# Another order of places for the first expert-row gathers, and what is moved for it

## The reference, cut to what matters

```
mod = silu(c) @ w_ada + b_ada                      # 6 vectors of 1024: ..., gate2 is the last
h2  = rms_norm(x, norm2_w) * (1 + scale2) + shift2
per token and head (8 heads): q = h2 @ peer_wq     # 2 halves of 128
  s = scores of each half against 128 keys; top 16 of each half
  combo = top16_a + top16_b (16 x 16); top 16 of it -> 16 expert numbers, g = softmax
  u_sel, v_sel = peer_u[expert], peer_v[expert]    # rows of 1024 each
  a = gelu(u_sel . h2);  y += sum_k (g * a)_k v_sel_k
x = x + gate2 * y
```

## Time and profile before

| | |
|---|---|
| median of 3 runs | 1178.29 us (1177.71 to 1179.69) |
| the profiled execution | 1180.36 us, its span 1178.4 us |
| TensorE, VectorE, ScalarE, POOL busy | 89%, 71%, 37%, 23% of the span |
| gathers (queue q0) | 36864 packets, 268.45 MB, 55.0% of the 16 engines' span |
| mean granted TensorE clock | 0.972 |

### The profile page before, as it was taken

One profiled execution on the slowest core, in us unless ns is written; L12 is line 12 of the kernel. 1 busy time (PEld: TensorE's weight loads), 2 busy tenths in 40 slices (PEclk: granted clock), 3 DMA queues, 4 the chain that ended last, 5 costly groups with the idle time before them and its releaser, 6 DMA issues.

```text
span 1178.4 us, 18884 instructions
## 1 busy us (share of the span) xinstructions
PE 1051.1 (89%) x7587; PEld 980.2 (83%) x7587; DVE 837.5 (71%) x1801; ACT 433.0 (37%) x913; POOL 268.8 (23%) x289
## 2 busy tenths in 40 slices
PE   8999987999999987777877778878999999999997
PEld 6999986998899877777877777778899888898886
DVE  7978889667667667666776766655756868765776
ACT  3635832123212221222122122211557654476452
POOL 1000005343334333333333333434000000300000
PEclk9999999999999999998999999989999999999999
DMA  9965988999999999999999999999854655455540
GB/s 371 406 244 180 348 313 307 420 421 420 421 420 420 421 420 421 420 421 420 420 420 421 420 421 422 420 422 420 325 208 161 237 205 184 147 211 179 186 171 36
DMA packets 59480, 390.35 MB, mean 331 GB/s; under 512 B 6785, under 2 KB 7809, under 8 KB 15618
## 3 DMA queue, kind: packets, MB, share of 16 engines
q0 software_dynamic: 36864, 268.45, 55.0%
q1 hardware_dynamic: 21056, 120.10, 27.8%
q10 hardware_dynamic: 1474, 0.60, 0.2%
HBM read 388.08 MB, written 1.05 MB: 330 GB/s over the span
## 4 chain that ended last, share of the span: by engine, by line
PE 63%; DMA 24%; DVE 6%; ACT 4%; issue 1%; SPq 0%; another core or an unknown queue 0%; DVEq 0%; ACTq 0%
DMA rows<-in_peer_uv,work 23%; PE aux L1566 23%; PE pj L1609 6%; PE pj L1611 5%; PE pj L1610 5%; PE aux L1545 5%; PE pj L1286 5%; PE pj L1287 4%; PE pj L1288 4%; DVE rows L2061 2%; DMA rows<-in_w_ada 1%; PE aux L1360 1%; ACT work L1142 1%; ACT rows L1010 1%; PE aux L1425 1%
## 5 line engine op out<-in xcount | busy, mean ns | idle before, releaser
L1566 PE MATMUL aux<-work,rows 128*128 128x128 f32 x2080 | 263.4, 291 | 73.8 <-ACT work L1142 73.8
L1566 PEld LDWEIGHTS aux<-work,rows 128*128 128x128 f32 x2080 | 256.2, 206 | 81.6 <-ACT work L1142 81.4
L1566 PE MATMUL aux<-work,low_pairs 128*128 128x128 f32 x2016 | 238.2, 279 | 30.2 <-ACT work L1142 30.1
L1566 PEld LDWEIGHTS aux<-work,low_pairs 128*128 128x128 f32 x2016 | 233.0, 195 | 34.0 <-ACT work L1142 34.0
L898 POOL DMA_INDIRECT rows<-in_peer_uv,work x130 | 125.5, 965 | 301.2 <-PE aux L1566 232.1
L707 DVE TENSOR_TENSOR wlo<-wring,whi 128x1024 fp32r<-128x1024 f32 x100 | 121.0, 1235 | 77.6 <-ACT whi L701 77.1
L898 POOL DMA_INDIRECT low_pairs<-in_peer_uv,work x126 | 118.3, 939 | 158.5 <-PE aux L1566 153.4
L1286 PE MATMUL pj<-xh,whi 128*128 128x256 f32 x512 | 146.3, 286 | 0.4
L1137 ACT ACTIVATE work<-work 128x4 f32<-128x4 f32 (+2 forms) x71 | 14.7, 207 | 358.3 <-DVE work L2061 358.3
L1287 PE MATMUL pj<-xl,whi 128*128 128x256 f32 x512 | 144.8, 283 | 0.0
L1288 PE MATMUL pj<-xh,wlo 128*128 128x256 f32 x512 | 144.8, 283 | 0.0
(11 more groups left out here) (288 smaller groups left out, 1461.5 us busy)
## 6 DMA issues: line engine op xcount, KB each, us to landing
wring<-in_w SPq DMA_DIRECT2D x76, 1024.0 KB, 4.8
rows<-in_w_ada SPq DMA_DIRECT2D x40, 512.0 KB, 10.1
low_pairs<-in_w_ada SPq DMA_DIRECT2D x1, 4096.0 KB, 13.4
rows<-in_w SPq DMA_DIRECT2D x3, 1024.0 KB, 10.4
rows<-in_peer_uv,work POOLq DMA_INDIRECT x130
work<-in_late_rows SPq DMA_DIRECT2D x2, 1024.0 KB, 7.5
xT<-in_gate_rows SPq DMA_DIRECT2D x2, 1024.0 KB, 7.2
rows<-in_norm_rows SPq DMA_DIRECT2D x2, 1024.0 KB, 7.3
```

The source lines that it names most:

```text
L1566: ins = mm(peer_sum[t][:, c * P:(c + 1) * P], pair(n)[:, D + c * P:D + (c + 1) * P], diag[:, n % PICKS, :], start=(n % (EXPERT_HEADS * PIC ...
```

## The change

Every pick gets its place from `slot(n)`. For picks before 240 it is the table FIRST_ORDER, the same permutation in each round of 12: picks 0 to 11 lie in places 0, 1, 6, 7, 2, 3, 4, 8, 9, 10, 11, 5. From pick 240 (`LAST_ROUND`) on it is n % 12 as before. POOL waits, before a pick from 12 on, for the latest earlier pick in the same place (`pick_ahead_in_slot`), and before the first twelve for what their place held: pick 4 for head 0's query, 5 for head 1's, 6 for the key scores of head 1, 7 to 10 for two, four, six and eight of the gate2 tiles, 11 for all of them.

`EARLY_HEADS = 2`: head 1's first tile is computed like head 0's, directly behind it and behind the transposes of h2 (`early_scores_of(1)`); `score_query` and `score_keys` of heads 0 and 1 then compute the second tile alone. VectorE's order becomes route(0), route(1), two gate2 tiles, and then in group 0: after each of the first four dot products one tile, after `weigh` the last two tiles, after the second `weigh` the bias. ScalarE's exponential of group 0 moves from behind head 1's scores to between the query and the scores of head 0's second tile, that of group 1 before the query of head 2.

```diff
--- before.py
+++ after.py
@@ -46,7 +46,7 @@
 LOW_PLACES = 8
 SLOTS, LOW_SLOTS = 12, 6
 PAIRS = SLOTS - LOW_SLOTS
-AHEAD = 2
+AHEAD, EARLY_HEADS = 2, 2
 EXPERTS = 4
 
 
@@ -265,6 +265,21 @@
 LOW_PICKS = LAST_PICK // SLOTS * SLOTS
 WHI_PICKS, WLO_PICKS, XH_PICKS, XL_PICKS = [LOW_PICKS - LOW_SLOTS + n for n in (2, 4, 5, 6)]
 LAST_GROUP = NT * EXPERT_HEADS - 1
+
+FIRST_ORDER = (0, 1, 6, 7, 2, 3, 4, 8, 9, 10, 11, 5)
+LAST_ROUND = LAST_PICK // SLOTS * SLOTS - SLOTS
+
+
+def slot(n):
+
+    return n % SLOTS if n >= LAST_ROUND else FIRST_ORDER[n % SLOTS]
+
+
+def pick_ahead_in_slot(n):
+
+    return max(m for m in range(n - 2 * SLOTS, n) if m >= 0 and slot(m) == slot(n))
+
+
 assert LAST_PICK % SLOTS < PAIRS
 GROUPS_BEFORE = [0]
 for g in range(NT * EXPERT_HEADS):
@@ -433,11 +448,11 @@
         own_place = {OWN_UNIT: own_unit, HELD_QUERY: low_pairs[:, 7, :]} | {n: low_pairs[:, 6, 512 * i:512 * i + 512] for i, n in enumerate(SUB_UNITS)} | \
             {n: flat[:, FIRST_HEADS_AT + 2 * D * i:FIRST_HEADS_AT + 2 * D * i + AT_1[n + 1] - AT_1[n]] for i, n in enumerate(FIRST_HEADS)}
         LAST_ADA = 5 * KC
-        LAST_ADA_SLOT = PAIRS - 1
+        FIRST_QUERY_SLOTS, KEYS_SLOT, CONDITION_SLOT, LAST_ADA_SLOTS = (2, 3), 4, 5, tuple(PAIRS + n for n in range(2, 6))
 
         def pair(n):
 
-            k = n % SLOTS
+            k = slot(n)
             return rows[:, k, :] if k < PAIRS else low_pairs[:, k - PAIRS, :]
 
 
@@ -811,10 +826,10 @@
                 for n in range(N2):
                     unit = N1 + l * N2 + n
                     if l == 0 and n == 1:
-                        sp.wait_ge(pair_loaded[(LAST_PICK - 2) % SLOTS], 16 * ((LAST_PICK - 2) // SLOTS + 1))
+                        sp.wait_ge(pair_loaded[slot(LAST_PICK - 2)], 16 * ((LAST_PICK - 2) // SLOTS + 1))
                     if l == 0 and n == 2:
                         load_rows(vg_rows.rearrange("p l f -> p (l f)"), "vg_rows", 0, vg_rows_loaded)
-                        sp.wait_ge(pair_loaded[LAST_PICK % SLOTS], 16 * (LAST_PICK // SLOTS + 1))
+                        sp.wait_ge(pair_loaded[slot(LAST_PICK)], 16 * (LAST_PICK // SLOTS + 1))
                     if l == 0 and n == 4:
                         sp.wait_ge(routed, NT * EXPERT_HEADS)
                         sp.wait_ge(gate_exp, NT * EXPERT_HEADS)
@@ -887,18 +902,21 @@
                 pool.wait_ge(routed, g + 1)
                 for j in range(PICKS):
                     n = g * PICKS + j
-                    if n in (2, 3):
-                        pool.wait_ge(queries, 2 * n - 2)
-                    if n == 4:
+                    k = slot(n)
+                    if n >= SLOTS:
+                        pool.wait_ge(pair_used, pick_ahead_in_slot(n) + 1)
+                    elif k in FIRST_QUERY_SLOTS:
+                        pool.wait_ge(queries, 2 * FIRST_QUERY_SLOTS.index(k) + 2)
+                    elif k == KEYS_SLOT:
                         pool.wait_ge(expert_scores, 2)
-                    if n == LAST_ADA_SLOT:
+                    elif k == CONDITION_SLOT:
                         pool.wait_ge(last_ada_used, KC)
-                    if n >= SLOTS:
-                        pool.wait_ge(pair_used, n - SLOTS + 1)
+                    elif k in LAST_ADA_SLOTS:
+                        pool.wait_ge(last_ada_used, 2 * LAST_ADA_SLOTS.index(k) + 2)
                     pool.indirect_dma_start(
                         out=pair(n), out_offset=None, in_=a["peer_uv"],
                         in_offset=bass.IndirectOffsetOnAxis(ap=expert[g % EXPERTS][:, j:j + 1], axis=0)) \
-                        .then_inc(pair_loaded[n % SLOTS], 16)
+                        .then_inc(pair_loaded[k], 16)
 
             pool.iota(distance, pattern=[[-1, T]], base=P, channel_multiplier=1).then_inc(bias_iota, 1)
             pool.wait_ge(bias_lin, HEADS)
@@ -1092,7 +1110,7 @@
 
             def score_query(h):
 
-                ts = slice(P if h == 0 else 0, T)
+                ts = slice(P if h < EARLY_HEADS else 0, T)
                 for s in range(2):
                     act.wait_ge(queries, 2 * h + s + 1)
                     if h >= 2:
@@ -1102,28 +1120,36 @@
             def score_out(h):
 
                 act.wait_ge(expert_scores, h + 1)
-                first = 1 if h == 0 else 0
+                first = 1 if h < EARLY_HEADS else 0
                 nc.scalar.copy(s_all[:, h + first * EXPERT_HEADS::EXPERT_HEADS, :],
                                aux[:, h % 2, first * 2 * KEYS:].rearrange("p (n k) -> p n k", k=2 * KEYS)).then_inc(scores_out, 1)
 
+            def early_head(h):
+
+                for s in range(2):
+                    act.wait_ge(early_query, 2 * h + s + 1)
+                    nc.scalar.copy(pq[:, h, s, 0:P], aux[:, 4 + s, 0:P]).then_inc(early_query_out, 1)
+                act.wait_ge(early_scores, h + 1)
+                nc.scalar.copy(s_all[:, h, :], aux[:, h, 0:2 * KEYS]).then_inc(early_scores_out, 1)
+
             shift(0)
-            for s in range(2):
-                act.wait_ge(early_query, s + 1)
-                nc.scalar.copy(pq[:, 0, s, 0:P], aux[:, 4 + s, 0:P]).then_inc(early_query_out, 1)
-            act.wait_ge(early_scores, 1)
-            nc.scalar.copy(s_all[:, 0, :], aux[:, 0, 0:2 * KEYS]).then_inc(early_scores_out, 1)
+            early_head(0)
             shift(1)
+            early_head(1)
 
             def gate_exps(g):
 
                 act.wait_ge(routed, g + 1)
                 nc.scalar.activation(gate[g % EXPERTS], top, ACT.Exp, bias=negtop, accum_out=gate_sum[g % EXPERTS]).then_inc(gate_exp, 1)
 
-            for h in range(AHEAD + 1):
-                score_query(h)
-                score_out(h)
-                if h:
-                    gate_exps(h - 1)
+            score_query(0)
+            gate_exps(0)
+            score_out(0)
+            score_query(1)
+            score_out(1)
+            gate_exps(1)
+            score_query(2)
+            score_out(2)
             def x0_hi(t):
 
                 for c in range(2):
@@ -1553,7 +1579,9 @@
                 pe.wait_ge(queries_out, 2 * h + 2)
                 if h >= 2:
                     pe.wait_ge(scores_out, h - 1)
-                for t in range(1 if h == 0 else 0, NT):
+                if h < EARLY_HEADS:
+                    pe.wait_ge(early_scores_out, h + 1)
+                for t in range(1 if h < EARLY_HEADS else 0, NT):
                     for s in range(2):
                         ins = mm(aux[:, h % 2, (2 * t + s) * KEYS:(2 * t + s + 1) * KEYS], pq[:, h % 2, s, t * P:(t + 1) * P],
                                  w[:, 0, (2 * (h % 2) + s) * KEYS:(2 * (h % 2) + s + 1) * KEYS], start=True, stop=True)
@@ -1567,21 +1595,22 @@
                              start=(n % (EXPERT_HEADS * PICKS) == 0 and c % 4 == 0), stop=False, skip_group_check=True)
                 ins.then_inc(pair_used, 1)
 
-            def early_scores_of_head_0():
-
-                w_wait(pe, UNITS_1.index(queries_of(0)))
-                w = w_slot(UNITS_1.index(queries_of(0)))
+            def early_scores_of(h):
+
+                w_wait(pe, UNITS_1.index(queries_of(h)))
+                w = w_slot(UNITS_1.index(queries_of(h)))
                 for s in range(2):
                     for k in range(KC):
-                        if s == 0:
+                        if h == 0 and s == 0:
                             pe.wait_ge(h_ready, KC + k + 1)
                         ins = mm(aux[:, 4 + s, 0:P], w[:, k, s * P:(s + 1) * P], hT[:, k, 0:P], start=(k == 0), stop=(k == KC - 1))
                     ins.then_inc(early_query, 1)
                 n = UNITS_1.index(keys_of(0))
                 w_wait(pe, n)
                 for s in range(2):
-                    pe.wait_ge(early_query_out, s + 1)
-                    ins = mm(aux[:, 0, s * KEYS:(s + 1) * KEYS], pq[:, 0, s, 0:P], w_slot(n)[:, 0, s * KEYS:(s + 1) * KEYS], start=True, stop=True)
+                    pe.wait_ge(early_query_out, 2 * h + s + 1)
+                    ins = mm(aux[:, h, s * KEYS:(s + 1) * KEYS], pq[:, h, s, 0:P], w_slot(n)[:, 0, (2 * h + s) * KEYS:(2 * h + s + 1) * KEYS],
+                             start=True, stop=True)
                 ins.then_inc(early_scores, 1)
 
             def x_tile(l, t):
@@ -1612,12 +1641,12 @@
                     ins.then_inc(steps, 1)
 
             keep_busy(4, 1)
-            early_scores_of_head_0()
+            early_scores_of(0)
             pe.wait_ge(taken_dve, KC)
             turn_h2(0)
+            early_scores_of(1)
             pe.wait_ge(h_ready, 3 * KC)
             score_query(0)
-            pe.wait_ge(early_scores_out, 1)
             score_keys(0)
             for h in range(1, AHEAD + 1):
                 score_query(h)
@@ -1761,12 +1790,14 @@
                 dve.wait_ge(ada_used, hi)
                 chain.link(v.tensor_tensor(mod[:, lo:hi], mod[:, lo:hi], cols[:, B_ADA + lo:B_ADA + hi], ALU.add))
 
-            def last_ada_tiles():
+            def last_ada_tiles(lo, hi):
```

(21 more changed lines are left out.)

## The result

The changed kernel has a median of 1181.65 us (1179.68 to 1185.29) beside 1179.05 us (1177.56 to 1182.07) for the kernel before on the same chip. The ratio is 1.0022 with a 95% interval of 1.0016 to 1.0029: slower by 2.6 us (1.9 to 3.4) where 2.7 us less was forecast, and above the upper end of the range, 1180.0. Its profiled execution lasted 1180.01 us with a span of 1178.1 us; the one of before had 1180.36 and 1178.4. These two are single executions. They agree within 0.4 us though the medians are 2.6 apart, so the traces show where time went, and the medians how much.

A forecast was written before the change was run, and what follows sets the result against it. The gathers' DMA queue, at a 421 GB/s plateau, was taken to bound the kernel. Head gain -3.0 us and return to n % 12 +0.3 gave -2.7: median 1178.29 to 1175.6 us, range 1173.6 to 1180.0.

The forecast's parts named there:

- the return to `n % 12`: Tail, from pick 240: pick 245 waits for pick 239; cost taken as 0.3 us, between 0 and 5.8.
- rival B: Tail: the hole at pick 245 is dear, 5.8 us lost, net +2.8, so 1181.1 us; chance 0.10.
- Head gain: Start of the gathers: 0.94 us from earlier data plus 2.02 of recovered rate, rounded 3.0 us; bounds 0 and 4.7.
- Rival A: Head: the gain is smaller, 1.2 us less 0.3, so 1177.4 us, or 1178.3 if the first issue stays long; chance 0.35.
- a queue filled ahead of demand: Head: with picks issued before the queue needs them, 2.02 us of the losses recovered, a start-up loss of 0.95 staying.
- First issues: POOL's first gather issue beside route(1), not dot products: 0.94 us instead of 1.88, data 0.94 us earlier; bounds 0 and 0.94.
- Places without waits: Head: picks 0 to 3 need nothing, picks 4, 5, 6 go out at 184.8, 186.0, 187.4; queue covered until 199.6.
- Moved tiles: VectorE, gate2 tiles among group 0's dot products: places free in time by 4 us or more, cost nothing.
- The stall of 0.5 us: VectorE in route_pairs(1): waits for ScalarE's exponential of group 0, from about 182.4 to 182.9; cost 0.5 us.
- The queue's cover of 8.2 us: Gathers at pick 20's issue: the queue still had 8.2 us of work; said to stay near 8.
- rival C: TensorE becomes the bound, needing the stream to gain more than 8.2 us; chance below 0.03, time within the range.

The follow-up runs named there:

- changed, again: The changed kernel once more, unaltered: 1182.28 us, ratio 1.0020 against the kernel before.
- iota early: The changed kernel with POOL's iota issued at pick 240 and not behind pick 255: 1182.11 us, ratio 1.0019 against the kernel before.
- wait for 239 alone: The kernel before with only the waits of picks 242 to 245 as in the changed kernel, pick 245 waiting for pick 239: 1182.74 us, ratio 1.0025.
- wait for 237 alone: The kernel before with the changed waits of picks 242 to 244, but pick 245 waiting for pick 237: 1179.47 us, ratio 1.0008.
- wait for 235: The kernel before with the changed waits of picks 242 to 244, but pick 245 waiting for pick 235: 1179.64 us, ratio 1.0005.
- gradual: The changed kernel with its places led back to n % 12 by swaps of neighbours from round 8 to 13: 1178.13 us, ratio 0.9987 against the kernel before.
- early scores only: The changed kernel keeping only head 1's early scores; places, gate2 tiles and exponentials in the old order: 1178.83 us, ratio 0.9990 against the kernel before.
- gradual, again: The changed kernel with the return by swaps of neighbours, measured once more: 1178.87 us, ratio 0.9994 against the kernel before.
- places only: Of the change only the order of places, returned by swaps; head 1 scored as before, tiles between the routes: 1179.31 us, ratio 0.9998 against the kernel before.
- gradual, early iota: The changed kernel with the return by swaps of neighbours and POOL's iota issued early: 1177.40 us, ratio 0.9985 against the kernel before.
- gradual, early iota, again: The changed kernel with the return by swaps and the early iota, measured once more: 1178.24 us, ratio 0.9992 against the kernel before.
- return at 120: The changed kernel with the one-step return at pick 120 instead of 240, pick 125 waiting for pick 119: 1180.74 us, ratio 1.0006 against the kernel before.

## Why the prediction was wrong

**The step that failed is the return to `n % 12`**, taken at 0.3 us; it costs 2.9 us. The geometry was right, even in its numbers: the issue of pick 245 moved to where pick 239 is freed (804.06; 803 was forecast), the picks behind it followed at 1.24 us, and its issue ended 806.50 - 805.00 = 1.5 us ahead of the landing of 244, just as worked out. What was wrong is what 1.5 us are worth. The step let pick 245 land one 2.49 us behind pick 244 because its issue had ended ahead of 244's landing ("the last one sees no hole"), that is 0.94 + 1.5 + 2.49 = 4.9 us from the start of the issue to the landing. With most of the engines out of work it takes 5.5 to 5.8 us:

| kernel | pick 245 issued | due | ahead | landed | issue to landing | late | 243 to 247 |
|---|---|---|---|---|---|---|---|
| before | 793.99 | | | | | | 9.94 |
| changed | 804.06 | 808.99 | 4.9 | 809.67 | 5.6 | 0.7 | 12.1 |
| changed, again | 805.97 | 809.3 | 3.3 | 811.74 | 5.8 | 2.4 | 13.6 |
| iota early | 806.66 | 809.97 | 3.3 | 812.19 | 5.5 | 2.2 | 13.75 |
| wait for 239 alone | 805.55 | 809.0 | 3.4 | 811.27 | 5.7 | 2.3 | 13.4 |
| wait for 237 alone | 801.71 | 810.2 | 8.5 | 810.22 | in step | 0 | |

Due is the landing of pick 244 and 2.49 us. The issue must begin 5.5 to 5.8 us ahead of it; 4.9 is too short and 8.5 long enough.

The traces also hold the sixteen increments of each gather's semaphore, taken here as one from each DMA engine, since each of the sixteen keeps its own step of 2.48 us from gather to gather (a few records are missing):

| kernel | issue of 245 ends | 244: first to last increment | 245: first to last |
|---|---|---|---|
| before | 794.93 | 798.25 to 808.38 | 800.74 to 810.86 |
| changed | 805.00 | 800.67 to 806.48 | 809.17 to 809.64 |
| wait for 239 alone | 806.49 | 799.16 to 806.49 | 810.52 to 811.24 |

In the kernel before the quickest engine is 10.1 us ahead of the last one; the 4.4 us of rival B were a mean. With the wait all sixteen restart nearly together, and the first of them is done only 4.0 to 4.2 us behind the end of the issue, where its share of a gather takes 2.48 us in the stream. By that estimate some 1.6 us pass between the end of an issue and its first data, and the prediction left them out. Data moved again at about 806.7 in the changed kernel and 808.0 with the wait alone. The quickest engine had then stood for some 6 and 9 us, and the last one too had run dry, for 0.2 and 1.5 us; its own share then took 0.5 and 0.7 us longer than in the stream. Together that is the 0.7 and 2.3 us by which pick 245 is late.

The second part of the price is behind the restart: the picks after the restart don't land 2.49 us apart at once (in the changed kernel 2.90 and 3.56), so that pick 247 is late by 2.2 to 3.8 us in the four traces with the wait. The third is that nothing of this is hidden. The prediction counted 1.6 us as hidden because pick 255's dot product doesn't wait for its data at 837.39; but it stands behind the work that follows pick 247, which takes 21.5 us in the kernel before (815.85 to 837.39), 21.1 in the changed one (816.13 to 837.26) and 22.3 with the wait alone (817.42 to 839.74). What pick 247 is late, pick 255 is late too. By the landing itself there was less to hide in than 1.6 us: in the kernel before the last increment of pick 255 stands at 836.87, 0.5 us ahead of its dot product. The range for this step held the answer (0 to 5.8); the value in it was taken from the wrong end, with the reason just shown to be wrong. In the 4 us ahead of the new issue's data the wait alone leaves 57 GB/s of 421: nearly all engines stood still. Rival B was right in its kind and its place. That its time also fits (1181.1; 1181.65 measured) is luck: it added 5.8 us of loss to 3.0 of gain, where 2.9 and about 1 were found. It had a chance of 0.10. Its test could have been made in the trace of before, because the first gather of all had an empty queue too: by the earlier trace rows its 1.0486 MB can't have been moved before 184 + (1.0486 - 2 x 0.221)/0.397 = 185.5, and its last increment stands at 186.18, 6.4 us behind the start of its issue, 0.94 of them the longer issue.

**Head gain: the term was three times too large.** Forecast 3.0 us, found about 1. Counted as in the prediction (losses against 421 GB/s in 13 us from 2.2 us behind the first issue), the heads are:

| old order of VectorE | lost, us | new order | lost, us |
|---|---|---|---|
| before | 2.97 | changed | 0.6 |
| wait for 239 alone | 1.6 | changed, again | 1.07 |
| wait for 237 | 1.5 | iota early | 1.1 |
| wait for 235 | 1.6 | gradual | 1.2 |
| early scores only | 1.85 | gradual, again | 0.97 |
| places only | 2.0 | gradual, early iota | 1.1 |
| | | gradual, early iota, again | 1.1 |
| | | return at 120 | 0.65 |
| mean | 1.9 | mean | 0.97 |

The difference of the means is 0.95 us. The stretches are counted from the issue, so the earlier start of the data is in it. The last increment of pick 24, counted from the first issue, says the same: 71.0 us on the mean in the six traces of the old order and 70.0 in the eight of the new one. The term was mis-sized twice. The losses of one execution of before, 2.97 us, were taken as those of the kernel; the same head in the three versions with a wait lost 1.5 to 1.6, and where the earlier trace rows have 326 GB/s the one that waits for 239 had 387. From the first issue to pick 247 that execution of before took 636.06 us, the other four without a costly wait and with the old order 633.8 to 634.2. And the new head keeps 0.97 us of loss, where the forecast left it 2.97 - 2.96, nothing. Rival A, at 1.2 us, has the size, and the version with the gradual way back, which is the changed head without the dear wait, confirms it with 1.1 us.

How the 1 us divides is in part open. The prediction gave 2.02 of its 3.0 us to a queue filled ahead of demand; the version with the places alone has that order and gained nothing measurable, and head 1's early scores alone can't be told from the whole (0.9990 beside 0.9987). Only the shorter first issue, 0.71 us, is seen directly.

**First issues.** Forecast 0.94 us each and 1.24 apart from the first: the first took 1.17 in all eight traces of the new head (why 0.23 more than the others is open), the next 0.94 at 1.24 apart. The 1.88 us were indeed the company of the tiles; the first three are 1.88, 1.75 and 1.99 in every version that keeps the tiles there, and pick 6 of the changed kernel, issued at 190.63 beside a moved tile, took 1.62. What is behind these lengths is told in the last section. The Trainium skill (SBUF — State Buffer, Who interferes with whom) infers that a `tensor_tensor` with two SBUF inputs leaves the writing of descriptors alone. For an indirect gather, whose issue also reads the expert numbers from SBUF, these traces say otherwise, for L1768 and for plain `TENSOR_TENSOR` rows too; whether it is that read or the writing of descriptors that waits, no run shows.

**Places without waits.** Picks 0 to 4 needed none, as forecast. Pick 5 waited until 189.03 for head 1's query, which was forecast for 186.0 + 1.76 = 187.8; TensorE was later by that. It cost nothing in this trace: 418 and 414 GB/s stand in those stretches.

**Moved tiles.** With the 1.76 us by which the gathers began later in this execution, route(1) was to end at 190.2 and ended at 188.99 + 0.18 = 189.17; the first weigh was to be at 201.9 and came at 202.19; TensorE's sums at 202.8, and 202.90. The stall of 0.5 us didn't come. Picks 7 to 10 were issued at 192.56, 196.49, 201.07 and 204.97, within 1 us of the forecast, and VectorE waited for none of picks 7 to 11. The queue's cover of 8.2 us held in the long run (421 GB/s to 800), and rival C stayed away.

**The sum.** About 1 us gained at the head and 2.9 lost at the tail give +1.9 us; measured are +2.6 (1.9 to 3.4). The 0.7 between them is within what the two terms are uncertain by. The traces agree on the tail: from the first issue to pick 247 the four with the gradual way back took 632.8 to 634.0 us, 633.5 on the mean, and the three with the changed head and the wait 634.6, 636.7 and 637.5, or 2.8 more. What stays open: the first gather began at 179.68 to 182.78 us in these traces, and at 179.98 in one and 182.46 in another execution of one and the same version (the gradual way back); and the work behind pick 247 took 361.0 to 362.6 us in the traces without a costly wait and 362.0 to 363.4 in those with it. Such scatter is as large as the effects, is older than the changed code and isn't explained.

## What to carry to other kernels

When the order in which buffers are taken is changed and changed back, each buffer's distance in steps is what counts: look for the one step whose buffer is freed last, and everything queued behind it. A transfer on a queue that has run empty needs its whole way from issue to landing ahead of its due time, 5.5 to 5.8 us here for 1.05 MB, not the 2.49 us between two landings; a way back spread over rounds, with no buffer taken again under 11 picks of 12, cost nothing that could be measured. And the rate in a few us of one execution is a sample: before a dip is counted as a gain to be had, it should be seen in a second trace.

## What was not expected of the hardware

A dip of the rate without a loss, and a loss out of proportion to the wait: with pick 245 issued at 801.71 the stretch of 800 to 804 falls to 332 GB/s and the picks land in step; with the issue 4 us later the stretches have 215 and 57 GB/s and about 3 us are gone. The quick engines are out of work in both; only in the second the last one runs dry as well. The reason for so much room is a drift: in the trace of before the sixteen increments of one gather lie 0.4 us apart at pick 0, 2.6 at pick 24, 6.2 at pick 120 and 10.1 at pick 240. A hole sets the engines level again (0.7 us at pick 245 with the wait alone, 1.9 at pick 250). Behind such a hole the next two gathers land 6.1 to 6.6 us behind the first (816.13 - 809.67, 817.42 - 811.27, 817.91 - 811.74, 818.75 - 812.19) and not 4.98.

An indirect gather's issue on POOL that begins while VectorE runs an operation with both operands in SBUF stands until 0.13 us before that operation's end, and only then takes its usual time (0.94 us, 1.17 for the very first). So the first issue of before, at 179.79, stands for the rest of the L1768 that began at 179.41. All 32 issues in the fourteen traces that began beside such a multiply-and-sum of 128x1024 fit this within 0.02 us, and so do those that began in the middle of a plain `TENSOR_TENSOR` of 128x256 or 128x512, as in the kernel before:

```profile
195.70 0.69 DVE L2042 TENSOR_TENSOR work<-count,work 128x512 f32<-128x512 int32 x1
195.98 1.23 POOL L898 DMA_INDIRECT low_pairs<-in_peer_uv,work  x1 [0.30 <-issue]
```

The same multiply-and-sum with h2 in PSUM lengthened none of the more than 1,900 issues that began beside it. An issue that begins first isn't lengthened either: pick 7 of the changed kernel, at 192.56, took 0.94 though a tile began at 192.71. Of the 1 us that the head gained, 0.71 are the first issue (1.88 - 1.17).
